# Weight chunks by half the contraction, mixer pieces behind TensorE, and expert gates applied by ScalarE

## The chip, the cores and the metric

The kernel runs on one core of a Trainium2 chip, in float32. The metric is device time in microseconds (us). Of the engines, PE is TensorE, ACT is ScalarE, DVE is VectorE, POOL is GpSimd, and SP is SyncE, which here only issues loads and stores.

## What is computed

One decoder layer for a prompt of 1024 tokens and for 8 sample tokens, at width 1024. The token mixer runs 8 retention heads and 8 dilated attention heads side by side. The channel mixer (PEER) lets each of 8 product-key heads pick 16 of 16384 single-neuron experts for each token:

```python
sh1, sc1, gt1, sh2, sc2, gt2 = adaln(c, w_ada, b_ada)
h = rmsnorm(x, g_norm1) * (1 + sc1) + sh1
rq, rk, rv, rg, aq, ak, av = mixer_projections(h, w_in, g_qn, g_kn)
o_ret, o_att, state = core(rq, rk, rv, aq, ak, av)
x = x + gt1 * mixer_output(o_ret, rg, o_att, g_ret, w_out)
h2 = rmsnorm(x, g_norm2) * (1 + sc2) + sh2
# peer, for each token and head: 16 experts eidx with scores top_s
g = softmax(top_s)
a = gelu(einsum('thkd,td->thk', peer_u[eidx], h2))
x = x + gt2 * einsum('thk,thkd->td', g * a, peer_v[eidx])
```

The outputs are x for both groups, the final retention states, and the new keys and values.

## The kernel before, in words

`build` runs three parts one after the other: `condition` (the adaLN tables), `decode` (the sample tokens up to their PEER scores) and `layer` (the prompt, and PEER for the sample at the end). The change is in `layer` alone.

`layer` works on T = 8 tiles of 128 tokens. Two streams of work are woven into each engine's one instruction list.

The PEER stream is the clock of the weave. A tile has 8 heads (HP), a head 16 expert slots, and two slots are a group (GRP = 2), so a head has 8 groups, a tile 64 (STEPS), the kernel 512. For a slot, POOL gathers a row of u and v for each of 128 tokens into a ring buffer (128 x 2048 elements, 1 MB; RING = 8 slots, four groups). DVE takes the dot product of the u half with h2 (L1395). ACT applies gelu (L965). DVE multiplies in the gate and the inverse of the softmax sum (L1411). ACT scales the v half in place (L968). PE turns it and sums it over slots in PSUM (L1134), which frees the slot for POOL (semaphore `ring_free`). While group q of head n runs, DVE also does part q of choosing the experts of head n+2 (`choose_next`). The scores of head n + AHEAD are made by PE at q = 6 and copied by ACT at q = 7.

The mixer stream is `front()`, a generator on PE, ACT and DVE each. It is cut into pieces by `yield when(t, o)`. After each group an engine runs the pieces that are due (`pace.upto`). `when` gives the group in which piece position o of tile t is due: all of tile 0 before the first group, tile 1 at o // 2, tile t from 32 groups before the start of tile t-1 on. In one tile the positions run: norm 0 to 5, input projection 6 to 19 (14 chunks of w_in, one a group, c < NIN), retention 21 to 24, attention 23 to 52 (heads in pairs, 7 groups a pair), output projection 54 to 58 (4 chunks of w_out), norm and query projection 61 to 66 (4 chunks of w_pq), queries turned at 68. In a group PE's piece comes after its transposes of that group, ACT's after its scalings, DVE's after its dots.

A chunk of weights is [128, 8, 256], that is all of the contraction for 256 columns, in one of NB = 3 buffers. SP issues chunk i when chunk i-3 has been used (L749). Its list is fixed, with the stores and the other loads in between: `load_rows` waits for the end of attention (L762), `store_y` for the sum of a tile two back (L786). `product` (L986) multiplies a chunk by eight matmuls.

At the end, the sample's experts are stored and reloaded through DRAM to have them one to a partition: DVE finishes `gate_s` in group 1 of the last head, SP stores it (L838) and loads it back in 16 small pieces (L842), POOL casts the indices (L870), gathers eight more slots (L855), and DVE, ACT and PE finish `y_sample` (L1443 to L1455).

## Time and profile before

| | us |
|---|---|
| median of 3 runs | 3926.47 |
| lowest, highest | 3908.15, 3930.04 |
| the profiled execution | 3911.71 |
| its span, first to last instruction | 3909.9 |
| PE, DVE, ACT, POOL busy | 2641.9, 2331.0, 1770.7, 1122.8 |

The mixer of tile 0 starts at 276 us; the first group ends at 441 us, the last at 3878 us. The tiles of the PEER stream end at 958, 1388, 1827, 2262, 2705, 3159, 3540 and 3878 us. DMA share is the mean busy share of 16 DMA engines; it comes out slightly above 1 where they never rest. PEclk is the clock that PE was granted, as a part of its full 2.4 GHz. A wait in brackets, as [13.14 <-DMA ...], is idle time of the engine before the instruction and what ended it.

### The profile page before, as it was taken

The page shows a single profiled execution, that of the slowest core. Times are in us where ns is not written, and L with a number is a line of the kernel's source. Part 1 is how long each engine was busy: PE and PEld are TensorE (multiplying, and loading weights), DVE is VectorE, ACT ScalarE, POOL GpSimd, SP SyncE. Part 2 cuts the span into 40 slices and gives each one's busy share as a digit, 9 for nine tenths or more (in the row PEclk, how much of TensorE's full clock was granted, in tenths as well). Part 3 has the DMA queues.
Part 4 walks back from the last instruction along what each step waited for, and adds up shares of the span by engine and source line. Part 5 has one row for each costly group of instructions (what it writes and reads, how often), then busy time and mean ns, then how long its engine had stood idle before and what let it go on. Part 6 is the DMA issues. An engine that isn't in the chain of part 4 may idle for free.

```text
span 3909.9 us, 37947 instructions
## 1 busy us (share of the span) xinstructions
PE 2641.9 (68%) x13651; PEld 2177.5 (56%) x13651; DVE 2331.0 (60%) x5816; ACT 1770.7 (45%) x2366; POOL 1122.8 (29%) x1054
## 2 busy tenths in 40 slices
PE   8777575676666766676666776676756767655555
PEld 2236464575556655565555665566655656554543
DVE  0222545457765686557765676557755577576775
ACT  0101344445544554445544554545544465454553
POOL 0000222223422233223332233322322233243443
PEclk9888786788778787787788778887778878777787
DMA  7846797899999999899999999898989999899998
GB/s 270 284 150 195 297 334 272 310 377 359 414 355 379 359 402 405 310 387 354 413 369 361 350 400 383 329 385 340 382 331 366 359 367 378 326 421 418 415 415 331
DMA packets 383772, 1373.34 MB, mean 351 GB/s; under 512 B 35168, under 2 KB 215888, under 8 KB 250208
## 3 DMA queue, kind: packets, MB, share of 16 engines
q0 software_dynamic: 149072, 1083.68, 69.6%
q1 hardware_dynamic: 234512, 287.23, 21.6%
q8 instruction: 107, 1.75, 0.2%
q14 instruction: 81, 0.66, 0.0%
HBM read 1356.74 MB, written 14.09 MB: 351 GB/s over the span
## 4 chain that ended last, share of the span: by engine, by line
PE 32%; DMA 20%; DVE 19%; ACT 18%; issue 3%; POOL 1%; DVEq 0%; POOLq 0%
PE pairA L1134 15%; PE pairS L986 12%; ACT pr_ring L968 10%; DMA pr_ring<-uv,pr_expert 10%; DVE pr_ring L1395 9%; DMA pr_w<-w_in 4%; DMA pr_w<-w_out 3%; DMA pr_w<-w_pq 3%; PE pairT L992 2%; ACT L965 2%; DVE pr_act_h L1411 1%; PE pairS L1053 1%; ACT pr_act_h L965 1%; POOL pr_ring L855 1%; ACT pr_sp L922 1%
## 5 line engine op out<-in xcount | busy, mean ns | idle before, releaser
L1134 PE MATMUL pairA<-sb_ident,pr_ring 128*128 128x128 f32 x8192 | 1389.6, 341 | 1009.7 <-ACT pr_ring L968 1006.4
L1134 PEld LDWEIGHTS pairA<-sb_ident,pr_ring 128*128 128x128 f32 x8192 | 1251.8, 180 | 1156.4 <-ACT pr_ring L968 1125.2
L855 POOL DMA_INDIRECT pr_ring<-uv,pr_expert x1024 | 1099.7, 1074 | 2492.2 <-PE pairA L1134 2175.9
L1395 DVE CUSTOM_DVE_ANT_0 pr_ring<-pr_ring,pr_h 128x1024 f32<-128x1024 f32 x1024 | 1222.6, 1222 | 135.3 <-DMA pr_ring<-uv,pr_expert 118.1
L968 ACT ACTIVATE pr_ring<-pr_ring,pr_act_h 128x1024 f32<-128x1024 f32 x1024 | 1120.1, 1141 | 157.3 <-DVE pr_act_h L1411 157.3
L986 PE MATMUL pairS<-pr_w,pr_hT 128*128 128x256 f32 x2304 | 572.3, 407 | 101.9 <-DMA pr_w<-w_in 51.8
L965 ACT ACTIVATE pr_act_h<-pr_dot 128x2 f32<-128x2 f32 x512 | 104.6, 204 | 1111.1 <-DVE pr_dot L1395 1109.2
L986 PEld LDWEIGHTS pairS<-pr_w,pr_hT 128*128 128x128 f32 x2304 | 468.9, 208 | 177.3 <-DMA pr_w<-w_pq 46.3
L1411 DVE SCALAR_TENSOR_TENSOR pr_act_h<-pr_act_h,pr_gsum,pr_gate_h 128x2 f32<-128x2 f32 x512 | 113.2, 221 | 603.8 <-ACT pr_act_h L965 603.5
L986 PE MATMUL pairS<-pr_w,pr_turned 128*128 128x256 f32 x512 | 135.4, 426 | 51.9 <-DMA pr_w<-w_out 47.4
L965 ACT ACT_TABLE_LOAD x127 | 162.9, 1283 | 2.2
L986 PEld LDWEIGHTS pairS<-pr_w,pr_turned 128*128 128x128 f32 x512 | 109.5, 219 | 71.3 <-DMA pr_w<-w_out 48.8
L1053 PE MATMUL pairS<-pr_kTva,pr_turned 64*128 64x512 f32 (+3 forms) x192 | 95.9, 614 | 6.8 <-DVE pr_st L1224 6.8
L146 PE MATMUL pairT<-ad_w,ad_cT 128*9 128x512 f32 x192 | 86.5, 605 | 9.9 <-DMA ad_w<-w_ada 9.9
L1320 DVE TENSOR_TENSOR pr_qk<-pairS,pr_rows 128x512 f32<-128x512 f32 x16 | 11.1, 692 | 133.1 <-PE pairS L986 133.1
L1222 DVE CUSTOM_DVE_ANT_0 pr_sp<-pairS,pr_dist 128x128 f32<-128x128 f32 (+7 forms) x64 | 48.4, 757 | 63.5 <-PE pairS L1053 58.9
L1395 DVE DVE_READ_ACCUMULATOR2_ANT pr_dot<- 128x1 f32 x1024 | 84.3, 82 | 0.0
L958 ACT ACT_TABLE_LOAD x64 | 82.1, 1283 | 1.1
L1192 DVE COPY pr_qk<-pairS 128x512 f32<-128x512 f32 x16 | 11.1, 692 | 106.6 <-PE pairS L986 106.6
L1068 PE MATMUL bank<-pr_kTva,pr_pt 128*128 128x65 f32 x504 | 68.8, 285 | 3.0 <-DVE pr_pt L1232 3.0
L1068 PEld LDWEIGHTS bank<-pr_kTva,pr_pt 128*128 128x128 f32 x504 | 66.6, 206 | 7.0 <-DVE pr_pt L1232 5.6
L1338 DVE MAX8 pr_top<-pr_work 128x8 f32<-128x128 f32 (+2 forms) x195 | 65.7, 337 | 4.6
(276 smaller groups left out, 1965.2 us busy)
## 6 DMA issues: line engine op xcount, KB each, us to landing
pr_w<-w_in SPq DMA_DIRECT2D x112, 1024.0 KB, 14.8
pr_w<-w_out SPq DMA_DIRECT2D x32, 1024.0 KB, 26.3
pr_w<-w_pq SPq DMA_DIRECT2D x32, 1024.0 KB, 18.8
ad_w<-w_ada SPq DMA_DIRECT2D x12, 2048.0 KB, 7.9
pr_ring<-uv,pr_expert POOLq DMA_INDIRECT x1024, 9.7
de_w<-w_in SPq DMA_DIRECT2D x7, 2048.0 KB, 11.0
...
de_kv<-k_sel SPq DMA_DIRECT2D x4, 1024.0 KB, 11.8
```

What stands on the lines that cost most here:

```text
L146: last = pe.matmul(ps[c % 2][0:NC9, :], cT[:, k, :], w[c % WBUF][:, k, :], start=(k == 0), stop=(k == KT - 1))
L855: pool.indirect_dma_start(ring[r][:], None, a["uv"], bass.IndirectOffsetOnAxis(ap=index, axis=0)).then_inc(s_g[r], 16)
L958: act.activation(gate_h[u][:], delta[u][:], ACT.Exp, accum_out=gsum[u][:, 0:1]).then_inc(s_ge, 1)
L965: act.activation(act_h[:, c], dot[:, c], ACT.Gelu).then_inc(s_gelu, 1)
L968: last = act.activation(ring[s % RING][:, D:2 * D], ring[s % RING][:, D:2 * D], ACT.Identity, scale=act_h[:, s:s + 1])
L986: last = pe.matmul(psS[:, at:at + CW], lhs[:, k, :], w[i % NB][:, k, :], start=(k == 0), stop=(k == KT - 1))
L992: last = pe.transpose(psT[:, at + k * P:at + (k + 1) * P], src[:, k * P:(k + 1) * P], ident[:])
L1053: last = pe.matmul(psS[:, c], aqT[e, h // 2, :], kT[e, h // 2, c], start=True, stop=True)
L1068: last = pe.matmul(out, pt[:, k * P:(k + 1) * P], va[:, k, h * VA:(h + 1) * VA], start=(k == 0), stop=(k == t))
L1134: last = pe.matmul(psA[:, k * P:(k + 1) * P], ring[s % RING][:, D + k * P:D + (k + 1) * P], ident[:], start=(h == 0 and s == 0 and k % 4 = ...
L1395: last = dve.tensor_tensor_reduce(ring[r][:, 0:D], ring[r][:, 0:D], h2[t % 2][:], 1.0, 0.0, ALU.mult, ALU.add, dot[:, s:s + 1])
L1411: dve.scalar_tensor_tensor(out=act_h[:, c], in0=act_h[:, c], scalar=gsum[u][:, 1:2], in1=gate_h[u][:, c], op0=ALU.mult, op1=ALU.mult)\
```

## The change

Three edits in `layer`.

Weights: a chunk is now half of the contraction for 512 columns, [128, 4, 512], still 1 MB, so that a contiguous piece of a weight row is 2 KB instead of 1 KB. The two halves of the contraction are summed in PSUM by consecutive chunks. `product` issues four matmuls of 512 columns instead of eight of 256. Number and order of the chunks stay.

Places of the pieces: tile t starts 16 groups before the start of tile t-1 instead of 32, tile 1 is at o * 3 // 4 instead of o // 2, and the positions are new. Pieces of ACT and DVE that read a result of PE are placed two groups after the PE piece that makes it. In the order of before, and with the old ranges in brackets: PE norm 1 (5), input projection 3 to 16 (6 to 19), retention 18 to 20 (21 to 23), attention 20 to 39 (23 to 52), two groups a head and no longer in pairs, output projection 41 to 46 (54 to 58), query projection 50 to 55 (62 to 66), queries turned 57, read by ACT at 59 (both 68). AHEAD is 3 instead of 4.

Gates: ACT makes the exponentials of head n+1 at group 2 of head n, DVE normalises them at group 4 (new function `gates` on each). ACT then multiplies gelu's result by the gates itself, with one 128x1 operation for each slot (scale = the gate), and waits for its own results by semaphores. DVE's L1407 and L1411 and its waits for gelu are gone. The sum of a tile (`yT`, written over `qk`) has a new wait, for PE's turning of the next tile's `qk`. The gates of the sample are made by ACT at group 2 of the last head and by DVE at group 4, instead of before group 0 and at group 1.

The core of the diff:

```diff
-    AHEAD = 4
+    AHEAD = 3
+    LEAD = 16
...
-    CW = 256
+    CK = KT // 2
...
     def when(t, o):
 
-        return -1 if t == 0 else o // 2 if t == 1 else (t - 1) * STEPS - STEPS // 2 + o
+        return -1 if t == 0 else o * 3 // 4 if t == 1 else (t - 1) * STEPS - LEAD + o
...
-        w = [sb(f"w{i}", [P, KT, CW]) for i in range(NB)]
+        w = [sb(f"w{i}", [P, CK, 512]) for i in range(NB)]
...
@@ -739,13 +741,13 @@
                 t, c = i // NCH, i % NCH
                 if i >= NB:
                     spq.wait_ge(s_pj, i - NB + 1)
+                ks, half = slice(c % 2 * CK, c % 2 * CK + CK), (c - NIN) // 2 % 2
                 if c < NIN:
-                    at = ORDER[c // 2] * HW + (c % 2) * CW
-                    src = w_in[:, :, at:at + CW]
+                    src = w_in[:, ks, ORDER[c // 2] * HW:(ORDER[c // 2] + 1) * HW]
                 elif c < NIN + 4:
-                    src = w_out[:, :, (c - NIN) * CW:(c - NIN + 1) * CW]
+                    src = w_out[:, ks, half * 512:half * 512 + 512]
                 else:
-                    src = w_pq[:, :, (c - NIN - 4) * CW:(c - NIN - 3) * CW]
+                    src = w_pq[:, ks, half * 512:half * 512 + 512]
                 spq.dma_start(w[i % NB][:], src).then_inc(s_w[i % NB], 16)
...
@@ -1069,42 +1082,35 @@
                                              va[:, k, h * VA:(h + 1) * VA], start=(k == 0), stop=(k == t))
                         last.then_inc(s_pv, 1)
 
-                    for pair in range(4):
-                        p = 23 + 7 * pair
-                        yield when(t, p)
-                        scores(2 * pair)
-                        if pair >= 1:
-                            yield when(t, p + 1)
-                            weighted(2 * pair - 1)
-                        yield when(t, p + 2)
-                        scores(2 * pair + 1)
-                        yield when(t, p + 5)
-                        turn_probs(2 * pair)
-                        yield when(t, p + 6)
-                        weighted(2 * pair)
-                        turn_probs(2 * pair + 1)
-                    yield when(t, 52)
-                    weighted(H - 1)
-
-                    yield when(t, 54)
+                    scores(0)
+                    for h in range(1, H + 2):
+                        if h < H:
+                            yield when(t, 20 + 2 * h)
+                            scores(h)
+                        yield when(t, 21 + 2 * h)
+                        if h >= 2:
+                            weighted(h - 2)
+                        if h <= H:
+                            turn_probs(h - 1)
+                    yield when(t, 41)
                     pe.wait_ge(s_mix, t + 1)
...
@@ -1273,29 +1279,21 @@
                         dve.tensor_tensor(x[:].rearrange("p (h c) -> p h c", h=H)[:, :, 0:HD], heads(osb),
                                           heads(srg), ALU.mult).then_inc(s_gated, 1)
 
-                    for pair in range(4):
-                        p = 23 + 7 * pair
-                        yield when(t, p + 1)
-                        if pair == 0:
-                            ret_out()
-                            center()
+                    for h in range(H + 1):
+                        if h < H:
+                            yield when(t, 22 + 2 * h)
+                            if h == 0:
+                                ret_out()
+                                center()
+                            att_max(h)
+                        yield when(t, 23 + 2 * h)
+                        if h == 0:
+                            deviation()
                         else:
-                            att_weigh(2 * pair - 1)
-                        att_max(2 * pair)
-                        if pair == 0:
-                            yield when(t, p + 2)
-                            deviation()
-                        yield when(t, p + 3)
...
@@ -950,27 +951,39 @@
 
             pace = Pace(front())
             pace.upto(-1)
+            def gates(n):
+                act.wait_ge(s_top, n + 1)
+                act.activation(gate_h[n % 2][:], delta[n % 2][:], ACT.Exp,
+                               accum_out=gsum[n % 2][:, 0:1]).then_inc(s_ge, 1)
+
             for n in range(AHEAD):
                 scores_out(n)
+            gates(0)
             for n in range(N):
                 u = n % 2
-                act.wait_ge(s_top, n + 1)
-                act.activation(gate_h[u][:], delta[u][:], ACT.Exp, accum_out=gsum[u][:, 0:1]).then_inc(s_ge, 1)
-                if n == N - 1:
-                    act.wait_ge(s_tops, 1)
-                    act.activation(gate_s[:], delta_s[:], ACT.Exp, accum_out=gsum_s[:, 0:1]).then_inc(s_ges, 1)
+                act.wait_ge(s_gn, n + 1)
                 for q in range(GROUPS):
-                    act.wait_ge(s_dot, n * GROUPS + q + 1)
+                    j = n * GROUPS + q
+                    act.wait_ge(s_dot, j + 1)
                     c = slice(q * GRP, q * GRP + GRP)
                     act.activation(act_h[:, c], dot[:, c], ACT.Gelu).then_inc(s_gelu, 1)
-                    act.wait_ge(s_coef, n * GROUPS + q + 1)
+                    act.wait_ge(s_gelu, j + 1)
+                    for s in range(q * GRP, q * GRP + GRP):
+                        last = act.activation(act_h[:, s:s + 1], act_h[:, s:s + 1], ACT.Identity, scale=gate_h[u][:, s:s + 1])
+                    last.then_inc(s_coef, 1)
+                    act.wait_ge(s_coef, j + 1)
                     for s in range(q * GRP, q * GRP + GRP):
                         last = act.activation(ring[s % RING][:, D:2 * D], ring[s % RING][:, D:2 * D], ACT.Identity,
                                               scale=act_h[:, s:s + 1])
                     last.then_inc(s_dg, 1)
+                    if q == 2 and n + 1 < N:
+                        gates(n + 1)
+                    if q == 2 and n == N - 1:
+                        act.wait_ge(s_tops, 1)
+                        act.activation(gate_s[:], delta_s[:], ACT.Exp, accum_out=gsum_s[:, 0:1]).then_inc(s_ges, 1)
                     if q == 7 and n + AHEAD < N:
                         scores_out(n + AHEAD)
-                    pace.upto(n * GROUPS + q)
+                    pace.upto(j)
 
...
@@ -981,9 +994,10 @@
             def product(t, c, lhs):
                 i = t * NCH + c
                 pe.wait_ge(s_w[i % NB], 16 * (i // NB + 1))
-                at = (c % 4 if c < NIN else (c - NIN) % 4) * CW
-                for k in range(KT):
-                    last = pe.matmul(psS[:, at:at + CW], lhs[:, k, :], w[i % NB][:, k, :],
+                at = (c // 2 if c < NIN else (c - NIN) // 2) % 2 * 512
+                for j in range(CK):
+                    k = c % 2 * CK + j
+                    last = pe.matmul(psS[:, at:at + 512], lhs[:, k, :], w[i % NB][:, j, :],
                                      start=(k == 0), stop=(k == KT - 1))
                 last.then_inc(s_pj, 1)
...
@@ -1376,6 +1374,12 @@
                 if part == 7:
                     dve.tensor_copy(expert[u][:], expert_f[:]).then_inc(s_top, 1)
 
+            def gates(n):
+                u = n % 2
+                dve.wait_ge(s_ge, n + 1)
+                step(dve.reciprocal(gsum[u][:, 1:2], gsum[u][:, 0:1]))
+                dve.tensor_scalar(gate_h[u][:], gate_h[u][:], gsum[u][:, 1:2], None, ALU.mult).then_inc(s_gn, 1)
+
             PARTS = 8
             assert PARTS == GROUPS
             pace = Pace(front())
@@ -1384,6 +1388,8 @@
             for n in range(2):
                 for part in range(PARTS):
                     choose_next(part, n)
+                if n == 0:
+                    gates(0)
 
             for n in range(N):
                 t, h, u = n // HP, n % HP, n % 2
@@ -1395,34 +1401,29 @@
                         last = dve.tensor_tensor_reduce(ring[r][:, 0:D], ring[r][:, 0:D], h2[t % 2][:], 1.0, 0.0,
                                                         ALU.mult, ALU.add, dot[:, s:s + 1])
                     last.then_inc(s_dot, 1)
-                    if q == 0:
-                        if h == 0 and t >= 1:
-                            dve.wait_ge(s_free, n * GROUPS)
-                            dve.wait_ge(s_owk, 16 * min(t + 2, T))
-                            if t >= T - 1:
-                                dve.wait_ge(s_oxm, 16 * T)
-                            dve.tensor_tensor(yT, psA[:].rearrange("p (k i) -> p k i", k=KT),
-                                              tabs[:, 5, :, B:B + 1].to_broadcast([P, KT, P]), ALU.mult).then_inc(s_yT, 1)
-                        dve.wait_ge(s_ge, n + 1)
-                        step(dve.reciprocal(gsum[u][:, 1:2], gsum[u][:, 0:1]))
-
-                    dve.wait_ge(s_gelu, n * GROUPS + q + 1)
-                    c = slice(q * GRP, q * GRP + GRP)
-                    dve.scalar_tensor_tensor(out=act_h[:, c], in0=act_h[:, c], scalar=gsum[u][:, 1:2],
-                                             in1=gate_h[u][:, c], op0=ALU.mult, op1=ALU.mult)\
-                       .then_inc(s_coef, 1)
+                    if q == 0 and h == 0 and t >= 1:
+                        dve.wait_ge(s_free, n * GROUPS)
+                        if t + 1 < T:
+                            dve.wait_ge(s_T, 15 * (t + 1) + 2)
+                        dve.wait_ge(s_owk, 16 * min(t + 2, T))
+                        if t >= T - 1:
+                            dve.wait_ge(s_oxm, 16 * T)
+                        dve.tensor_tensor(yT, psA[:].rearrange("p (k i) -> p k i", k=KT),
+                                          tabs[:, 5, :, B:B + 1].to_broadcast([P, KT, P]), ALU.mult).then_inc(s_yT, 1)
+                    if n + 2 < N:
+                        choose_next(q, n + 2)
                     if q == 0 and h == 0 and t >= 1:
                         dve.wait_ge(s_xmid, 16 * t)
                         dve.wait_ge(s_yb, t)
                         dve.tensor_tensor(xmid[:], psA[:], xmid[:], ALU.add).then_inc(s_out, 1)
-                    if n + 2 < N:
-                        choose_next(q, n + 2)
+                    if q == 4 and n + 1 < N:
+                        gates(n + 1)
                     if n == N - 2:
                         choose(q, ROWS_S, sc_s, delta_s, expert_s)
                         if q == GROUPS - 1:
                             dve.sem_inc(s_tops, 1)
                             dve.sem_inc(s_gts, 1)
-                    if n == N - 1 and q == 1:
+                    if n == N - 1 and q == 4:
                         dve.wait_ge(s_ges, 1)
                         step(dve.reciprocal(gsum_s[:, 1:2], gsum_s[:, 0:1]))
                         dve.tensor_scalar(gate_s[:], gate_s[:], gsum_s[:, 1:2], None, ALU.mult).then_inc(s_gts, 1)
```

## Rows read from the trace of the kernel before

**Rows 1.** Page, parts 1, 2, 3 and 6: busy, slices, queues, one issue
```profile
PE 2641.9 (68%) x13651; PEld 2177.5 (56%) x13651; DVE 2331.0 (60%) x5816; ACT 1770.7 (45%) x2366; POOL 1122.8 (29%) x1054
...
DMA  7846797899999999899999999898989999899998
...
q0 software_dynamic: 149072, 1083.68, 69.6%
...
q1 hardware_dynamic: 234512, 287.23, 21.6%
...
pr_w<-w_out SPq DMA_DIRECT2D x32, 1024.0 KB, 26.3
```

**Rows 2.** Windows: length, busy of PE, PEld, DVE, ACT, POOL; PEclk, DMA share, GB/s
```profile
276.00:441.00 165.00, 116.76 (x504) 96.03 (x504) 57.02 (x169) 29.28 (x54) 7.77 (x8) 0.77 0.64 216
441.00:958.00 517.00, 351.33 (x1854) 308.19 (x1855) 289.81 (x738) 232.60 (x316) 130.45 (x126) 0.79 0.89 330
958.00:3540.00 2582.00, 1751.44 (x9611) 1543.17 (x9611) 1687.34 (x4223) 1302.72 (x1713) 818.69 (x768) 0.79 0.96 371
3540.00:3878.00 338.00, 186.53 (x1044) 165.62 (x1042) 239.14 (x595) 175.91 (x229) 145.80 (x127) 0.76 0.99 405
```

**Rows 3.** Windows, shorter stretches, same columns
```profile
0.00:60.00 60.00, 50.06 (x127) 11.20 (x128) 0.00 (x0) 5.06 (x8) 0.20 (x4) 1.00 0.89 319
1705.00:1770.00 65.00, 54.33 (x316) 49.16 (x316) 37.34 (x92) 32.19 (x44) 17.60 (x19) 0.87 1.02 385
1549.00:1594.00 45.00, 27.05 (x117) 23.93 (x118) 25.09 (x56) 19.23 (x25) 10.82 (x10) 0.66 0.88 321
1777.00:1817.00 40.00, 25.93 (x138) 22.63 (x137) 32.18 (x81) 21.02 (x24) 11.70 (x12) 0.72 0.79 289
3560.00:3800.00 240.00, 128.70 (x726) 114.19 (x724) 173.66 (x439) 125.91 (x163) 109.94 (x91) 0.77 1.01 415
```

**Rows 4.** Timeline 1595 to 1636 us: start, us, instruction [idle before <-releaser]
```profile
1595.35 0.37 SPq L749 DMA_DIRECT2D pr_w<-w_pq  x1
...
1620.61 6.14 PE L986 MATMUL pairS<-pr_w,pr_hT 128*128 128x256 f32 x16 [13.14 <-DMA pr_w<-w_pq]
...
1626.79 0.60 ACT L939 ACTIVATE pr_sp<-pairS 128x512 f32<-128x512 f32 x1 [18.29 <-PE pairS L986]
...
1627.51 0.22 DVE L1411 SCALAR_TENSOR_TENSOR pr_act_h<-pr_act_h,pr_gsum,pr_gate_h 128x2 f32<-128x2 f32 x1 [16.97 <-ACT pr_act_h L965]
...
1635.22 0.20 ACT L883 ACTIVATE pr_st<-pr_st 128x1 f32<-128x1 f32 x1
```

**Rows 5.** Lines by form: busy us, mean ns | idle before, releaser
```profile
L968 ACT ACTIVATE pr_ring<-pr_ring,pr_act_h 128x1024 f32<-128x1024 f32 x1024 | 1120.1, 1141 | 157.3 <-DVE pr_act_h L1411 157.3
...
L965 ACT ACT_TABLE_LOAD x127 | 162.9, 1283 | 2.2
...
L1411 DVE SCALAR_TENSOR_TENSOR pr_act_h<-pr_act_h,pr_gsum,pr_gate_h 128x2 f32<-128x2 f32 x512 | 113.2, 221 | 603.8 <-ACT pr_act_h L965 603.5
...
L1222 DVE CUSTOM_DVE_ANT_0 pr_sp<-pairS,pr_dist 128x1024 f32<-128x1024 f32 x8 | 9.8, 1225 | 9.4 <-PE pairS L1053 8.1 <-issue 1.3
```

**Rows 6.** Timeline of PE in the last tile's attention
```profile
3121.85 3.78 PE L1053 MATMUL pairS<-pr_kTva,pr_turned 64*128 64x512 f32 x4
...
3125.56 3.67 PE L1134 MATMUL pairA<-sb_ident,pr_ring 128*128 128x128 f32 x16
...
3155.20 1.98 PE L1053 MATMUL pairS<-pr_kTva,pr_turned 64*128 64x512 f32 x4
...
3157.11 1.97 PE L1134 MATMUL pairA<-sb_ident,pr_ring 128*128 128x128 f32 x16
...
3158.91 1.90 PE L1068 MATMUL bank<-pr_kTva,pr_pt 128*128 128x65 f32 x16
```

**Rows 7.** Timeline at the end, SP and POOL
```profile
3843.16 0.47 SPq L838 DMA_DIRECT2D gate_s<-pr_gate_s  x1
...
3873.70 0.19 POOL L870 CAST pr_expT<-pr_expT_f 128x8 uint32<-128x8 f32 x1 [12.70 <-DMA pr_gateT<-gate_s]
```

80 lines of the change are left out of this document (37 added, 43 removed).

## The prediction

> **What bounds the kernel now.** I read the page's slices and queues first. The 16 DMA engines are at nine tenths in nearly every slice after the fifth, while no compute engine is above 68% over the span [rows 1]. Two queues share them: the gathers of expert rows (1083.68 MB, 69.6% of the span) and SP's queue with the weights (287.23 MB, 21.6%) [rows 1]. Then the windows by stage. The last tile of tokens runs almost without mixer work: 338 us for 64 groups, 5.28 us each, at a DMA share of 0.99 and 405 GB/s; an inner stretch of it gives 1.01 and 415 GB/s, which is what a full DMA looks like here [rows 2, 3]. The six tiles before it take 2582 us at 0.96, the first 517 us at 0.89 [rows 2]. So there are two costs to take away: idle DMA time (4% of 2582 us and 11% of 517 us, 103 + 57 = 160 us against a share of 1.00), and DMA time spent badly on small packets. Everything else can gain only through these.
>
> Where the DMA idles is seen inside the second tile: 1549 to 1594 us at 0.88 (output and query products), 1777 to 1817 at 0.79 (start of attention), while the input product, at 1705 to 1770, has 1.02 [rows 3]. One stall shows how it comes about [rows 4]. SP issues a chunk of w_pq at 1595.35. PE has nothing to do without it for 13.14 us and starts the product at 1620.61, 25 us after the issue. ACT stands in its own piece, waiting 18.29 us for that product, and DVE stands 16.97 us at L1411 for ACT's gelu. Meanwhile nobody frees a ring slot, and when the four groups in the ring have landed the DMA has only weights. Over the run DVE waits 603.5 us at L1411 in 505 places [rows 5].
>
> **The change part by part.**
>
> *Weight chunks.* A chunk stays 1 MB, but its packets are 2 KB, not 1 KB. SP's queue costs 0.216 x 3909.9 = 844.5 us for 287.23 MB, 2.94 us per MB, a mean that holds larger packets too. Weights with 2 KB packets are seen in the first 60 us: 0.89 x 60 us for 319 GB/s x 60 us = 19.1 MB, 2.79 us per MB [rows 1, 3]. The least saving is 0.15 us per MB on the 184.5 MB of the 176 chunks, 28 us. If the queue's other 103 MB cost 2.6, between that and the gathers' 0.696 x 3909.9 / 1083.68 = 2.51, the 1 KB packets cost 3.13 and the saving is 0.34, 62 us. I take 0.25 us per MB or 0.26 per chunk: it lies between, since the other 103 MB have small pieces too. 118 chunks fall in the six tiles (five times 22, and 8), 36 in the first: 30 + 9 us. The 22 of the opening stretch count nothing: the DMA share is 0.64 there [rows 2].
> The same edit changes when a chunk lands. Median landing of w_out is 26.3 us although 1 MB needs 3 us of the engines [rows 1]; that fits engines taking packets of the two queues in turn, each small one waiting for a large one. Half as many packets then wait half as often: I estimate 13 to 16 us for the 25 us of [rows 4]. The chunk is wanted three groups after its issue, 3 x 5.2 = 16 us, so the stalls of PE nearly go.
> The Trainium skill (DMA: Bandwidth & Descriptors, Queues, rings and completion order) says that an engine goes round the queues at packet granularity; the landing time agrees. The same page (Specifications) puts line rate at 512 B and more, by which 1 KB packets have nothing to gain; the rows, 2.94 against 2.79 us per MB, speak mildly against it. It is a rival below.
> PE's work per chunk stays: half the matmuls, each twice as long. The weight loads halve, but they run beside the matmuls (56% and 68% of the span, together over 100% [rows 1]): nothing.
>
> *Gates in ScalarE.* DVE loses 512 x 0.221 us = 113 us and the 603.5 us of waiting [rows 5]. It is not bound: about 72% busy without mixer work (173.66 of 240 us [rows 3]). What it gains is that a late ACT no longer holds up DVE's next dots or its mixer piece. ACT gains two 128x1 operations per group; nearest row 0.20 us each [rows 4]. It used to stand 157.3 / 512 = 0.31 us there for DVE [rows 5]. The chain from dots to scaled values is then gelu + 0.40 + two short waits on itself, against gelu + 0.31. Bounds: -0.1 us (they overlap) to +0.5 us per group. At the path it is nothing at either end, because gathers queue: a slot's data is awaited by a DMA at 0.99 and not by ACT. Without that cover 0.5 x 512 would be 256 us. The softmax sum is applied one head ahead (groups 2 and 4), with no more table loads.
>
> *Pieces two groups behind.* PE's piece of a group comes after its transposes, so ACT and DVE, who are ahead, waited for it in the same group. Now the readers sit two groups (10.6 us) later. Attention takes 20 groups for 30 and the whole mixer 59 for 68. Is there room? Per head and two groups, at 128 x 1024: DVE has 3.7 x 2 (72% of 5.28, twice) + 1.225 for the maximum [rows 5] + as much for the weighing, of the same shape + 0.2 = 10.1 us. ACT has 2 x (0.2 + 0.4 + 2.2) + 1.14 + two table loads of 1.283 = 9.3 (each head's exponential now changes the table by itself, where two shared a change). PE at full clock has 2 x 1.97 + 1.98 + 1.0 + 1.90 = 8.8 [rows 6]. The DMA needs 2 x 5.28 = 10.6, and more where w_out is loaded. It fits, narrowly for DVE in the last tile. Queued behind each moved piece are that engine's next dots, scalings or transposes; the ring of four groups covers some 10 us. SP's store_y finds its tile ready earlier (group 16 for 32), so the w_out loads behind it come earlier, into the attention stretch that idles now. The new DVE wait, for PE's turning of qk before yT is written over it, is on a piece due six groups before: nothing. AHEAD 3 for 4 leaves ACT's scores one group and more ahead of DVE: nothing.
> I take that the six tiles reach a share of 0.99: (2582 x 0.96 - 30) / 0.99 = 2449 / 0.99 = 2474, -108 us. The first tile has a mixer pressed into 44 groups, of which two per three stay on time: share 0.97, (517 x 0.89 - 9) / 0.97 = 465, -52 us. The last tile is full already: 0.
>
> *Start and end.* At the start choose(1) now waits for the first gates (a table load, 1.28, and small operations, some 2 us), against 2 us that larger packets may give between products: 0. At the end the sample's gates are made at group 4 of the last head instead of group 1. Their store (3843.16) begins the chain to POOL's cast at 3873.70, where POOL stood 12.70 us idle [rows 7]; the sample's eight gathers and the end of the kernel hang on it. Three groups x 5.28 = 15.8 later; the gathers no longer share the DMA: +14, bounds +10 and +16.
>
> *Sum.* -108 - 52 + 14 = -146. The profiled execution took 3911.7 us, so 3765.7. It is 0.4% below the median of the three runs, 3926.5, and near their lowest; I keep to it: **3765 us**.
>
> **The rivals.**
> 1. *Packets gain nothing*, since the engines move 1 KB pieces as fast as larger ones. The 39 us stay: 2479 / 0.99 = 2504 (-78), 460 / 0.97 = 474 (-43), +14: **3805**. (That is what the line rate of the Trainium skill's DMA page would give.) For it: the difference in rows is small and the 2 KB stretch has no gathers beside it.
> 2. *New waits for old.* Chunks still land late, because the alternation is only inferred, or DVE's 10.1 of 10.6 us makes late groups in attention. Half the idle time comes back: shares 0.975 and 0.92, 2449 / 0.975 = 2512 (-70), 451 / 0.92 = 490 (-27), +14: **3829**.
> 3. *The reordering does nothing*: shares as now, only packets, -39 + 14: **3887**, which is faster by 0.6% and with packets at their least (-22 + 14) no change. Against it: the stall of [rows 4] is plainly one of order and landing.
> 4. *Slower: PE at its low clock in the denser attention.* The granted clock averages 0.77 to 0.79 [rows 2], a mix of the two levels 2.4 and 1.2 GHz; the same 16 transposes take 1.97 or 3.67 us [rows 6]. At the low level a head of the last tile costs PE 3.78 + 1.8 + 3.8 + 2 x 3.67 = 16.8 us in two groups against 10.6 of DMA; with keys growing by tile the excess sums to about 19 us per head position, 154 us over eight heads. If then also the stalls stay, 3887 + 154 = **4041**; I put it at 3980. It decides the sign where PE's two groups average above 10.6 + 146 / 48 = 13.6 us over the six upper tiles. Against it: in [rows 6] PE is at the full level when its pieces follow each other without a gap, and the change makes them denser.
>
> **How the numbers follow.** Forecast 0.62, rival 1 0.10, rival 2 0.18, rival 3 0.04, rival 4 0.06. The predicted time is the forecast's. Its own range: shares 1.01 and 1.00 with 62 us of packets, (2479 - 41) / 1.01 = 2414 and 447, -168 - 70 + 12 gives 3686; the upper end is rival 1, 3805. The whole range takes rival 2 with some of its spread: **3690 to 3850**. A measurement can tell about 0.5% from no change, 20 us. Faster by more than that: 0.62 + 0.10 + 0.18 and half of rival 3, 0.90 with a little off for what I don't see; same 0.04; slower 0.06.
>
> **What would show it.** DMA share of the six middle tiles at 0.98 or more, with under 2474 + 20 us for them; median landing of w_out under 18 us; PE's waits on weights far under the present ones; ACT's wait on projections gone; DVE's wait on gelu gone with nothing of its size in its place; the sample's gathers some 15 us later against the last group. I am wrong if the share stays at 0.96, if landing stays near 26 us, if SP's cost per MB doesn't fall, or if PE's 3.67 us transposes fill the attention stretches.

## The result

The changed kernel takes 3596.31 us in the median of four runs (3593.3 to 3606.4); the kernel before, measured beside it, 3917.31 us (3902.18 to 3930.04). The ratio is 0.9186, 95% interval 0.9143 to 0.923: 321 us, or 8.1%, faster. Forecast were 3765 us and a range of 3690 to 3850, so the sign is right and the size is not: the gain is twice the one predicted, and the time lies 94 us below the range.

The page of the kernel after has the same parts as [rows 1]: busy time, the DMA's slices, the queues (packets, MB, share of 16 engines' span), and the median landing of the weight chunks, with two groups of ScalarE that the change touches.

```profile
span 3591.5 us, 35730 instructions
...
PE 2546.8 (71%) x12243; PEld 1797.8 (50%) x12243; DVE 2251.8 (63%) x5368; ACT 2046.4 (57%) x3415; POOL 1168.4 (33%) x1054
...
DMA  8736699999999999999999999999999999999998
...
q0 software_dynamic: 149072, 1083.68, 73.6%
q1 hardware_dynamic: 144400, 287.23, 21.7%
...
L972 ACT ACTIVATE pr_act_h<-pr_act_h,pr_gate_h 128x1 f32<-128x1 f32 x1024 | 245.8, 287 | 16.9
L969 ACT ACT_TABLE_LOAD x136 | 174.5, 1283 | 16.2 <-DVE pr_dot L1401 13.8
...
pr_w<-w_in SPq DMA_DIRECT2D x112, 1024.0 KB, 17.5
pr_w<-w_out SPq DMA_DIRECT2D x32, 1024.0 KB, 20.4
pr_w<-w_pq SPq DMA_DIRECT2D x32, 1024.0 KB, 23.6
```

The bytes are the same, 1083.68 and 287.23 MB; q1 moves them in 144400 packets where [rows 1] has 234512. In time, q0 is 0.736 x 3591.5 = 2643 us (before 0.696 x 3909.9 = 2721) and q1 0.217 x 3591.5 = 779 us (before 844.5). What is left of the span, when the two queues' time is taken off, is 169 us where it was 344; I call it idle time. So the 318 us between the two spans are three things: the DMA is less idle (175), the weights' packets cost less (65), and the gathers' packets, of which the change touches none, cost less too (78).

The windows by stage answer to [rows 2]: opening stretch, first tile, six middle tiles, last tile, end; columns as there.

```profile
276.00:439.00 163.00, 113.14 (x328) 59.61 (x328) 56.42 (x166) 28.39 (x51) 7.63 (x8) 0.78 0.64 221
439.00:865.00 426.00, 313.41 (x1478) 218.60 (x1477) 270.09 (x662) 263.65 (x443) 138.90 (x126) 0.84 1.00 398
865.00:3222.00 2357.00, 1690.63 (x8756) 1281.43 (x8754) 1642.26 (x3913) 1516.05 (x2508) 860.08 (x769) 0.83 1.00 406
3222.00:3560.00 338.00, 194.65 (x1042) 173.43 (x1042) 225.30 (x535) 207.74 (x356) 143.26 (x127) 0.73 0.99 405
3560.00:3592.00 32.00, 17.64 (x41) 3.39 (x40) 15.74 (x28) 1.62 (x8) 4.58 (x5) 0.87 0.64 256
```

The six tiles fell from 2582 to 2357 us and from 0.96 to 1.00, the first from 517 to 426 and from 0.89 to 1.00. The last tile is 338 us in both kernels and the opening stretch is 2 us shorter. From the first group to the last the kernel now moves 398 to 406 GB/s.

The table of waits (engine, line, what it waited for: total us, times, longest us) shows who waits in a kernel that the DMA bounds. First the kernel before, then the kernel after.

```profile
POOL pr_ring L855 <- PE pairA L1134: 2175.9, 499, 18.6
...
DVE pr_ring L1395 <- DMA pr_ring<-uv,pr_expert: 118.1, 127, 2.7
...
PE pairS L986 <- DMA pr_w<-w_in: 51.8, 15, 7.9
...
PE pairS L986 <- DMA pr_w<-w_out: 47.4, 6, 12.6
...
PE pairS L986 <- DMA pr_w<-w_pq: 44.9, 6, 13.1
```

```profile
POOL pr_ring L857 <- PE pairA L1140: 1806.2, 466, 20.1
ACT pr_act_h L969 <- DVE pr_dot L1401: 958.6, 379, 16.1
...
DVE pr_ring L1401 <- DMA pr_ring<-uv,pr_expert: 658.9, 519, 5.4
...
PE pairS L1000 <- DMA pr_w<-w_in: 139.9, 41, 6.7
...
PE pairS L1000 <- DMA pr_w<-w_pq: 31.9, 7, 5.6
...
PE pairS L1000 <- DMA pr_w<-w_out: 29.0, 7, 6.5
```

DVE's wait for ScalarE's gelu, 603.5 us in [rows 5], is gone. In its place DVE waits 658.9 us for the gathered rows themselves (118.1 before), in 519 places with 5.4 us at most: the first compute engine on a row stands ready before the data, and the DMA does not idle for it. PE's waits for weights are not gone. In total they have grown, from 144 us in 27 places to 201 us in 55; but no single one is over 6.7 us, against 13.14 in [rows 4].

### The profile page after: what moved, and what is told of

Same layout as the page of the kernel before. It is cut to its first block, busy times and chain, and to the rows that moved or that the text cites. A ratio compares the mean times of both kernels' runs of the same rounds, so it can differ in the third digit from the quotient of the medians.

```text
span 3591.5 us, 35730 instructions
## 1 busy us (share of the span) xinstructions
PE 2546.8 (71%) x12243; PEld 1797.8 (50%) x12243; DVE 2251.8 (63%) x5368; ACT 2046.4 (57%) x3415; POOL 1168.4 (33%) x1054
## 3 DMA queue, kind: packets, MB, share of 16 engines
q0 software_dynamic: 149072, 1083.68, 73.6%
q1 hardware_dynamic: 144400, 287.23, 21.7%
## 4 chain that ended last, share of the span: by engine, by line
DMA 42%; PE 23%; ACT 12%; DVE 9%; POOL 4%; issue 3%; POOLq 0%; DVEq 0%; ACTq 0%
DMA pr_ring<-uv,pr_expert 23%; PE pairS L1000 12%; DMA pr_w<-w_in 12%; PE pairA L1140 9%; ACT pr_ring L976 6%; DVE pr_ring L1401 5%; POOL pr_ring L857 4%; DMA pr_w<-w_pq 3%; DMA pr_w<-w_out 3%; ACT pr_act_h L972 1%; ACT L969 1%; ACT L923 1%; ACT pr_act_h L969 1%; PE pairT L1006 1%; PE bank L1081 0%
## 5 line engine op out<-in xcount | busy, mean ns | idle before, releaser
L857 POOL DMA_INDIRECT pr_ring<-uv,pr_expert x1024 | 1146.5, 1120 | 2129.6 <-PE pairA L1140 1806.2
L1140 PE MATMUL pairA<-sb_ident,pr_ring 128*128 128x128 f32 x8192 | 1286.3, 324 | 733.7 <-ACT pr_ring L976 723.2
L1401 DVE CUSTOM_DVE_ANT_0 pr_ring<-pr_ring,pr_h 128x1024 f32<-128x1024 f32 x1024 | 1242.2, 1224 | 671.1 <-DMA pr_ring<-uv,pr_expert 658.9
L1140 PEld LDWEIGHTS pairA<-sb_ident,pr_ring 128*128 128x128 f32 x8192 | 1167.6, 170 | 918.8 <-ACT pr_ring L976 843.1
L1000 PE MATMUL pairS<-pr_w,pr_hT 128*128 128x512 f32 x1152 | 594.5, 667 | 180.0 <-DMA pr_w<-w_in 139.9
L969 ACT ACTIVATE pr_act_h<-pr_dot 128x2 f32<-128x2 f32 x512 | 104.1, 203 | 960.1 <-DVE pr_dot L1401 958.6
L1000 PEld LDWEIGHTS pairS<-pr_w,pr_hT 128*128 128x128 f32 x1152 | 238.3, 216 | 455.1 <-issue 339.4
L972 ACT ACTIVATE pr_act_h<-pr_act_h,pr_gate_h 128x1 f32<-128x1 f32 x1024 | 245.8, 287 | 16.9
L1000 PE MATMUL pairS<-pr_w,pr_turned 128*128 128x512 f32 x256 | 132.6, 669 | 31.2 <-DMA pr_w<-w_out 29.0
L1000 PEld LDWEIGHTS pairS<-pr_w,pr_turned 128*128 128x128 f32 x256 | 52.9, 216 | 92.6 <-issue 58.3
L1337 DVE FIND_INDEX8 pr_pos<-pr_top,pr_work 128x8 uint32<-128x128 f32 (+2 forms) x195 | 64.2, 329 | 0.0
L1006 PE MATMUL pairT<-sb_ident,pr_sp 128*128 128x128 f32 x352 | 58.8, 302 | 5.7 <-ACT pr_sp L923 5.0
## 6 DMA issues: line engine op xcount, KB each, us to landing
pr_w<-w_in SPq DMA_DIRECT2D x112, 1024.0 KB, 17.5
pr_w<-w_out SPq DMA_DIRECT2D x32, 1024.0 KB, 20.4
pr_w<-w_pq SPq DMA_DIRECT2D x32, 1024.0 KB, 23.6
```

The source lines that it names most:

```text
L857: pool.indirect_dma_start(ring[r][:], None, a["uv"], bass.IndirectOffsetOnAxis(ap=index, axis=0)).then_inc(s_g[r], 16)
L969: act.activation(act_h[:, c], dot[:, c], ACT.Gelu).then_inc(s_gelu, 1)
L972: last = act.activation(act_h[:, s:s + 1], act_h[:, s:s + 1], ACT.Identity, scale=gate_h[u][:, s:s + 1])
L1000: last = pe.matmul(psS[:, at:at + 512], lhs[:, k, :], w[i % NB][:, j, :], start=(k == 0), stop=(k == KT - 1))
L1006: last = pe.transpose(psT[:, at + k * P:at + (k + 1) * P], src[:, k * P:(k + 1) * P], ident[:])
L1140: last = pe.matmul(psA[:, k * P:(k + 1) * P], ring[s % RING][:, D + k * P:D + (k + 1) * P], ident[:], start=(h == 0 and s == 0 and k % 4 = ...
```

## The experiments

Two theories of the gathers' cheaper packets are to be told apart. By the one (theory B in the expectations below) they are served faster because the weights' packets between them are fewer and larger; by the other (theory A) because the DMA has fewer gaps. The other questions are what each part is worth alone and beside the others, why the sum was too small, and why the tail's +14 us is missing.

Of each experiment the profiled span P is split as above: q0 and q1 are their shares times P, the rest is P less both. The packet times are means of the packet records in each trace, in ns: a gather packet of 8 KB, and a packet of a weight chunk with its size. P is one execution. That of e_places was the slowest of its four, 17 us above their median, that of e_1kb 8 us above, so their rest is high by up to so much. Gains in us below are differences of the ratios times 3917, unless other numbers stand there, because the kernels ran on several chips.

```
kernel            ratio   95% interval      P       q0    q1   rest  gather  weight packet
before            1                         3909.9  2721  845  344   327.9   49.6 (1 KB)
after             0.9186  0.9143 to 0.923   3591.5  2643  779  169   318.6   88.6 (2 KB)
e_chunks          0.9747  0.9694 to 0.9799  3818.1  2711  787  320   326.6   2 KB
e_places          0.9572  0.9528 to 0.9616  3766.3  2678  844  245   322.9   1 KB
e_gates           0.9957  0.9924 to 0.9991  3907.4  2716  844  348   327.5   1 KB
e_places_gates    0.949   0.9448 to 0.9532  3709.9  2656  842  212   320.1   1 KB
e_chunks_places   0.9143  0.9093 to 0.9194  3605.1  2661  779  166   320.5   2 KB
e_chunks_gates    0.966   0.9608 to 0.9711  3807.8  2707  784  316   326.5   2 KB
e_1kb             0.9493  0.9417 to 0.9568  3735.5  2656  848  231   319.9   49.8 (1 KB)
e_512b            0.9748  0.9671 to 0.9824  3822.7  2668  963  191   321.3   29.8 (512 B)
e_ring3           0.9796  0.9693 to 0.9899  3834.0  2764  786  284   333.2   2 KB
e_nolag           1.1828  1.1736 to 1.192   4641.8  2767  784  1091  333.6   2 KB
```

**Each part alone.** Three kernels, each the kernel before with one of the three parts of the change. Chunks (e_chunks):

```diff
-        w = [sb(f"w{i}", [P, KT, CW]) for i in range(NB)]
+        w = [sb(f"w{i}", [P, CK, 512]) for i in range(NB)]
...
-                    src = w_out[:, :, (c - NIN) * CW:(c - NIN + 1) * CW]
+                    src = w_out[:, ks, half * 512:half * 512 + 512]
```

> The kernel before with one part of the change: weight chunks of half the contraction by 512 columns, 2 KB packets. Places of pieces and gates as before. Theory A (gaps): the change gained mostly by closing gaps in the DMA's work, and gather packets took 329 ns on average instead of 318 because the DMA ran empty now and then; then this kernel keeps most gaps, gather packets stay above 325 ns, and it gains 40 to 90 us, around 3850. Theory B (contention): the 1 KB packets slow the gathers beside them; then gather packets fall to about 318 ns here already, and it gains 140 us or more, 3780 or less.

It took 3815.87 us, ratio 0.9747: 99 us faster, a little more than theory A allowed (40 to 90), and well short of theory B's 140. q1 fell by 58 us, q0 by 10, the rest by 24. The gathers' packets stay at 326.6 ns, though the weights' packets beside them are now 2 KB. So larger weight packets beside them are not what makes the gathers cheaper. With the old places the median landing of w_out falls to 19.6 us and that of w_pq to 15.4.

Places (e_places): the positions of all pieces on PE, ACT and DVE as in the diff, with AHEAD 3; chunks and gates as before.

```diff
-                    yield when(t, 54)
+                    yield when(t, 41)
                     pe.wait_ge(s_mix, t + 1)
```

> The kernel before with one part of the change: the new places of the mixer pieces (with AHEAD 3 and the wait before the sum of a tile). Chunks of 256 columns, gates multiplied in by DVE. Theory A: most of the gain is here, 150 to 220 us, around 3730, and the middle tiles reach a rate near 395 GB/s. Theory B: the stalls removed count for at most the idle share, about 100 us, 3815.

3751.52 us, ratio 0.9572: 168 us faster. Here q1 does not move (844 for 845) and the weights' packets are the old ones, but q0 falls by 43 us and the rest by 99. The gather packet falls from 327.9 to 322.9 ns in a kernel in which nothing was done to any packet. What this kernel changed is how seldom the DMA runs out of gathers. It does not say how the 168 us divide between the readers' distance of two groups, the denser attention and the later start: no kernel here has the distance with the old order.

Gates (e_gates): the gates multiplied in by ScalarE, with AHEAD 3 and everything else at its old place. In this kernel the scores of the last head of a tile are made from other queries than the reference's; the amount and the kind of the work are the same, only the rows that are gathered differ.

```diff
+                    act.wait_ge(s_gelu, j + 1)
+                    for s in range(q * GRP, q * GRP + GRP):
+                        last = act.activation(act_h[:, s:s + 1], act_h[:, s:s + 1], ACT.Identity, scale=gate_h[u][:, s:s + 1])
+                    last.then_inc(s_coef, 1)
```

> The kernel before with one part of the change: gates made one head ahead and multiplied in by ScalarE (with AHEAD 3, which it needs to start). Chunks and places as before. My account gives it little alone: ScalarE still stands waiting for TensorE in its pieces, so the slots are freed as late; DVE gains only its 1.2 us per group. 0 to 60 us, around 3885. A rival: DVE held up by ScalarE was the main cause of the gaps; then 120 us or more.

3910.58 us, ratio 0.9957, 0.9924 to 0.9991: 17 us at the most likely, and little more than can be told from nothing. Taking away DVE's 603.5 us of waiting for ACT gave no more than that, so these waits were hardly on the path.

**The parts in pairs.** 168 + 99 + 17 = 284 us, and the change, counted the same way, gives 319. Three more kernels leave one part out each.

> The changed kernel without its weight chunks: 256 columns and all of the contraction, 1 KB packets; places and gates as changed. Theory A: the DMA stays full, the gathers' packets stay at 318 to 320 ns, and only the packets of the weights cost more, 45 to 65 us: 3640 to 3665. Theory B: gather packets go back to 325 ns or more and it loses 120 us or more: 3720.

3714.31 us, ratio 0.949. Leaving the chunks out costs 119 us of the 319. The gather packets stay at 320.1 ns, as theory A has it and B (325 or more) has not. But A's price of 45 to 65 us was too low by half, and the time is nearly B's: q1 rises by 63 us, q0 by 13, and the idle time by 43. PE's waits on weights show where the last comes from.

```profile
PE pairS L999 <- DMA pr_w<-w_in: 199.8, 28, 13.3
...
PE pairS L999 <- DMA pr_w<-w_out: 92.3, 7, 14.2
...
PE pairS L999 <- DMA pr_w<-w_pq: 88.4, 7, 14.7
```

Together 380 us, the longest 14.7; in the kernel after they are 201 us and 6.7. With the denser places a chunk has less time before it is wanted. In 1 KB packets PE stands up to 14.7 us for one, once in each of seven tiles for w_out and for w_pq and 28 times for w_in.

> The changed kernel without its gates: DVE multiplies them in and waits for gelu again; chunks and places as changed. Without the chunks the gates were worth 37 us beside the new places. Theory A: about the same here, 25 to 45 us, 3630. Rival: with the DMA full there is nothing left for them, under 10 us, 3600.

3605.81 us, ratio 0.9143: the whole gain without the gates, as the rival had it. To compare it with the full change, both ran again on one chip.

> The changed kernel once more, to stand beside the next three on the same chip: 3590 to 3600, 0.915 to 0.922 of the kernel before.

> The changed kernel without its gates, once more beside it: the first time it stood at 0.914 on another chip, against 0.919 for the change. Theory A (with the DMA full, nothing is left for DVE and ACT to give): within 8 us of the changed kernel. Rival: 20 us or more slower, as the 37 us beside 1 KB packets say.

The full change took 3600.9 us, 0.9185 (0.9147 to 0.9222), the same without the gates 3607.78, 0.921 (0.9172 to 0.9248). The gates are worth 7 us there, inside both intervals. Where the DMA still idles they are worth more: 32 us beside the places alone (0.9572 to 0.949), and 34 beside the chunks alone (0.9747 to the 0.966 below).

The last pair keeps the old places. AHEAD is 4 again here, so that each tile's scores come from its own queries, and the first gates stand between the first score copies:

```diff
             for n in range(AHEAD):
                 scores_out(n)
+                if n == 1:
+                    gates(0)
```

> The changed kernel without its places: old positions and lead, AHEAD 4; chunks and gates as changed. Chunks alone gave 105 us, gates alone 17 us. If the parts add up: 3800, so that the places are worth 200 us on top of the others. If gates and chunks help each other (ACT and DVE no longer tied, chunks landing sooner), 3750 or less.

3808.23 us, ratio 0.966. The parts add up about as expected. Against the whole change this is 0.966 to 0.9186: the new places are worth some 185 us when the chunks and the gates are there, and 168 alone.

**The size of a weight packet.** The kernel after, with each chunk loaded in two column halves (packets of 1 KB) or four quarters (512 B). PE's work and every place stay.

```diff
-                spq.dma_start(w[i % NB][:], src).then_inc(s_w[i % NB], 16)
+                for s in range(2):
+                    cs = slice(s * 512 // 2, (s + 1) * 512 // 2)
+                    spq.dma_start(w[i % NB][:, :, cs], src[:, :, cs]).then_inc(s_w[i % NB], 16)
```

> The changed kernel with one thing back: each weight chunk is fetched by two loads of 256 columns into the same buffer, so its packets are 1 KB again; chunks, products, places and gates stay. Theory A: what the chunks gave is the packet size and nothing else, so it costs what the full undoing of the chunks cost, 118 us: 3700 to 3720, with SP's queue at about 840 us of the 16 engines and gather packets near 320 ns. Rival: half the contraction and TensorE's 512 columns gave a part; then it stays below 3680.

3729.12 us, ratio 0.9493. It is the same as e_places_gates with its 0.949, which has 1 KB packets in one load for each chunk: so the packets count, and neither the number of loads nor the shape of PE's product. Against the kernel after it is 120 us by the two ratios and 144 by the spans: q1 69, q0 13, rest 62 (43 in e_places_gates). The waits of PE for weights are twice those of the kernel after:

```profile
PE pairS L1002 <- DMA pr_w<-w_in: 224.5, 23, 13.9
...
PE pairS L1002 <- DMA pr_w<-w_pq: 94.8, 7, 14.7
PE pairS L1002 <- DMA pr_w<-w_out: 93.7, 7, 14.1
```

> As the last one, with four loads of 128 columns for a chunk, 512 B packets. From 49.6 ns at 1 KB and 88.6 ns at 2 KB a packet costs some 10.6 ns plus 38 ns per KB, so 30 ns at 512 B and 3.67 us per MB against 3.03: +118 us of DMA time above the 1 KB kernel, and more late chunks: 3830 to 3900. The rule that line rate begins at 512 B (the Trainium skill, DMA: Bandwidth & Descriptors, Specifications) would give the time of the 2 KB kernel, 3600.

3823.96 us, ratio 0.9748, with 272.0 + 116.7 + 105.9 = 495 us of such waits, the longest 17.7. q1 costs 115 us more than in e_1kb, and the kernel takes 100 more: part of it falls into idle time, which sinks from 231 to 191. So the columns of the table are no independent prices. A packet of 512 B takes 29.8 ns, of 1 KB 49.8, of 2 KB 88.6. A chunk of 1 MB on 16 engines then costs 3.82, 3.19 and 2.84 us with 2^20 bytes, or 3.64, 3.04 and 2.70 us for 10^6. The Trainium skill (DMA: Bandwidth & Descriptors, Specifications) puts line rate at 512 B and more. These runs disagree: between 512 B and 2 KB lie 35% in engine time and, by the ratios 0.9748 and 0.9186, 220 us of the kernel's. That was rival 1 of the prediction, and it falls.

**The distance between PE and its readers.** The kernel after, with the pieces of ACT and DVE moved back into the group of PE's piece that they read (two groups earlier, PE's places untouched).

```diff
                     for h in range(H):
-                        yield when(t, max(23, 22 + 2 * h))
+                        yield when(t, max(21, 20 + 2 * h))
                         act.wait_ge(s_nm, t * H + h + 1)
```

> The changed kernel with the pieces of ACT and DVE that read TensorE moved two groups forward, into the group of the TensorE piece that they read. TensorE's own places, the denser attention, the lead of 16 groups, chunks and gates stay. Theory A: the distance of two groups is what closes the gaps; it loses 80 to 150 us, 3700. Rival: the later start, the packing and the decoupled gates do it, and the ring covers such waits; under 30 us, 3620.

4642.73 us, ratio 1.1828: 716 us slower than before, 1035 slower than after. The sign was expected; the loss is some seven times the upper end that I wrote down. Its waits:

```profile
POOL pr_ring L857 <- PE pairA L1140: 2906.7, 451, 17.6
...
DVE pr_pt L1238 <- PE pairT L1006: 387.2, 64, 10.0
DVE pr_sp L1228 <- PE pairS L1066: 379.6, 53, 12.7
...
ACT pr_sp L923 <- DVE pr_st L1230: 272.4, 55, 8.0
```

64 and 53 times, once a head, DVE stands 6 to 7 us for PE, and ACT 5 us for DVE. In the stretch from 1700 to 1800 us the DMA share is 0.55 at 204 GB/s. The old order spread a pair of heads over seven groups; at two groups a head such waits come one behind the other. So the denser order pays only with the distance. That the ring's four groups cannot cover waits that come so close is my reading of it; no run changes the ring in this order.

**Gathers under way.** Does a gather's packet take longer because the DMA has gaps? The kernel after, with POOL allowed three groups in the ring and not four:

```diff
-                    if s % GRP == 0 and j >= RING // GRP:
-                        pool.wait_ge(s_free, j - RING // GRP + 1)
+                    if s % GRP == 0 and j >= RING // GRP - 1:
+                        pool.wait_ge(s_free, j - RING // GRP + 2)
```

> The changed kernel with three groups of gathers under way instead of four: POOL waits for one more freed group. No other change, packets of weights 2 KB. It tests whether gaps alone lengthen the gathers' packets: if so their mean rises from 318.6 ns to 325 ns or more while the time grows by over 100 us. If the mean stays at 318 to 320, the longer packets of the kernel before came from something else. The ring's cover goes too: I expect 3750 to 3900.

3843.86 us in the median of two runs, ratio 0.9796. Its queues, from the page, and a window in its last tile (same columns as the windows above):

```profile
q0 software_dynamic: 149072, 1083.68, 72.1%
q1 hardware_dynamic: 144400, 287.23, 20.5%
```

```profile
3560.00:3780.00 220.00, 118.78 (x580) 106.35 (x580) 128.18 (x307) 119.32 (x206) 83.79 (x73) 0.67 0.93 347
```

q0 is 0.721 x 3834.0 = 2764 us, 121 more than after, for the same bytes in the same packets, and the gather packet is 333.2 ns, above even the 327.9 of before, beside weight packets of 2 KB. In the window a share of 0.93 moves 347 GB/s, 2.68 us of DMA time per MB; the full stretch in [rows 3] moves 415 at 1.01, 2.43. So the busy share hides a loss: when fewer gathers are under way, the engines' records still show them busy, with longer packets. The total of idle time is not what sets it: e_ring3 has less than the kernel before (284 us for 344) and dearer packets, and e_nolag, with 1091, has no dearer ones than e_ring3.

The packet records say more than the means. The median gather packet takes 309 to 313 ns in every kernel of the table. What differs is how many take over 400 ns, some 700 on average: 1.26% after, 3.58% before, 2.50% in e_places, 5.14% in e_ring3, 5.21% in e_nolag. Without these the mean is 313.8 ns before and after alike, so they are all of the 78 us: what they cost above that mean is 117 us before and 39 after. They come where the engines had begun to run dry. From 400 to 3500 us of each run, of the gather packets that start when the 16 engines were less than 0.8 busy in the 400 ns before, 44 to 68 in 100 are long (after, before, e_ring3, e_nolag); of those that start at 0.97 or more, 1 to 3 in 100. From the first group to the last, the packets that start at less than 0.9 are 1.0% of the gathers after, 3.5% before, 5.4% in e_ring3 and 5.7% in e_nolag, the order of the means. So it goes by how often the engines run dry and not by how long. More than half of the long packets start at 0.9 or more all the same (in e_nolag just under half), and what delays those the records don't say.

**The tail.** The kernel after, with the sample's gates made at the first group of the last head:

```diff
-                    if q == 2 and n == N - 1:
+                    if q == 0 and n == N - 1:
...
-                    if n == N - 1 and q == 4:
+                    if n == N - 1 and q == 1:
```

> The changed kernel with the sample's gates made early again: ACT after group 0, DVE at group 1 of the last head. My prediction priced the later place at 14 us; in the changed trace the small loads behind it took 16.5 us from the store to POOL's cast, where they took 30.5 us before. Theory: those loads wait for the gathers' traffic to end either way, so this kernel is the same within 3 us, 3594 to 3599. If the price was real and hidden by something else, it gains 10 us or more.

3591.91 us, ratio 0.9103 (0.9052 to 0.9153): not to be told from the change itself. SP's timeline says why: first the kernel before, then the kernel after, then e_tail (start, us, instruction).

```profile
3848.77 4.51 SPq L842 DMA_DIRECT2D pr_expT_f<-expert_s  x8
3853.33 15.33 SPq L842 DMA_DIRECT2D pr_gateT<-gate_s  x8
```

```profile
3538.66 0.47 SPq L840 DMA_DIRECT2D gate_s<-pr_gate_s  x1
3544.53 3.74 SPq L844 DMA_DIRECT2D pr_expT_f<-expert_s  x8
3548.31 4.65 SPq L844 DMA_DIRECT2D pr_gateT<-gate_s  x8
```

```profile
3532.24 0.47 SPq L840 DMA_DIRECT2D gate_s<-pr_gate_s  x1
3538.12 3.66 SPq L844 DMA_DIRECT2D pr_expT_f<-expert_s  x8
3541.82 16.34 SPq L844 DMA_DIRECT2D pr_gateT<-gate_s  x8
```

The store is earlier, but the eight small loads of the gates then take 16.34 us to issue and not 4.65. They were as long before the change too (15.33 us). What the two slow cases have in common is that POOL still issues gathers of the prompt beside them (until 3551.8 in e_tail, 3861.0 before), while in the kernel after its last one is at 3544.1. It can't be the gathers alone, for the eight loads just ahead of them take 3.7 to 4.5 us in all three. POOL's cast, at the end of that chain, stands 5.9 us ahead of the last release of a slot in e_tail and 5.0 us ahead in the kernel after.

**Where the mixer of the next tile starts.** Most of the idle time that is left in the middle tiles lies at a tile's start. The windows at two of them in the kernel after:

```profile
2060.00:2100.00 40.00, 31.22 (x178) 23.07 (x179) 28.07 (x68) 20.48 (x35) 11.89 (x12) 0.87 0.78 304
...
2860.00:2900.00 40.00, 30.93 (x175) 22.66 (x176) 27.63 (x67) 20.48 (x35) 13.49 (x12) 0.87 0.81 309
```

0.78 and 0.81, where the windows of 40 us on both sides have 1.02. In the first of them a w_in chunk is late behind its predecessor, and the PEER work of every engine is queued behind it (start, us, instruction, idle before and what ended it):

```profile
2062.96 6.25 PE L1000 MATMUL pairS<-pr_w,pr_hT 128*128 128x512 f32 x8 [6.38 <-DMA pr_w<-w_in]
...
2070.19 1.22 DVE L1418 TENSOR_TENSOR pr_xmid<-pairA,pr_xmid 128x1024 f32<-128x1024 f32 x1 [12.35 <-PE pairA L1134]
```

L1134 and L1418 are the last steps of a tile of the PEER stream: its output is turned and added, which comes on top of the mixer's work when both fall in one group. With LEAD 18 or 20 for 16 the mixer's pieces stand two or four groups further from the tile's end.

```diff
-    LEAD = 16
+    LEAD = 18
```

> The changed kernel with a lead of 18 groups instead of 16, one number. In the changed trace three tiles begin with 53 to 55 us for 8 groups at a DMA share of 0.85 to 0.93, the others with 46 to 47: TensorE has the last two products of w_in just before and after turning the tile's sum, and waits for a late chunk with DVE and the ring behind it. With 18 these products come before the sum. If that is the cause, 10 to 25 us faster than the changed kernel; if the tile's end costs this anyway, within 5 us.

> The same with a lead of 20: the sum of a tile then falls in the first group of attention. If only the distance from the products counts, as e_lead18; if the heavy retention pieces at positions 20 to 22 meet the sum, slower than e_lead18 by 5 to 15 us.

On the chip of r_after (3600.9 us), LEAD 18 took 3587.42, ratio 0.9156 (0.912 to 0.9193), and LEAD 20 3589.87, 0.9153 (0.9116 to 0.919). Both came out as the distance from the products has it. The intervals overlap with r_after's, but they hold the noise of the kernel before; of the six runs of r_after on the same chip, five are above all six of LEAD 18 and all six of LEAD 20. So there is most likely a gain, and it is one of 11 to 13 us. The stretches in question, in e_lead18:

```profile
2020.00:2060.00 40.00, 29.99 (x135) 18.36 (x134) 11.90 (x21) 17.04 (x27) 10.64 (x10) 0.88 0.87 343
...
2820.00:2860.00 40.00, 31.20 (x131) 18.79 (x132) 12.72 (x24) 17.03 (x27) 9.70 (x10) 0.87 0.90 360
```

0.87 and 0.90, and a third at 0.91 near 2420: the gaps are shallower, but the picture is another one, for DVE is busy 12 us in these 40 where it was 28. So LEAD moves the stall and softens it; it doesn't take it away.

## Why the prediction was wrong

**Right.** The DMA bounds the kernel, and the gain came out of its idle time and its small packets. The last tile stayed at 338 us. ScalarE's extra work cost nothing at the path although I sized it too small: 0.48 us per group for the two 128x1 operations, 287 ns each in the page above, where I took 0.40 from the 0.20 of [rows 4] (that row's operation has no scale read from a tile). The Trainium skill (ScalarE: Activation LUTs, What ACT_TABLE_LOAD costs) adds some 93 ns for each operand that is read from a 128x1 tile; 287 ns against the 203 of the gelu at L969, a difference of 84, agrees. "Nothing of its size" in place of DVE's wait on gelu was a sign that failed, since 658.9 us of waiting for rows came, but they cost nothing. Rival 4 did not come: PEclk rose from 0.79 to 0.83 in the six tiles. My argument against it was weaker than I wrote, though: [rows 6] also has 3.78 and 3.67 us, at the low level, one right behind the other. Rival 3 falls with e_places (168 us from the reordering alone), rival 1 with e_1kb and e_512b, and rival 2 with the shares of 1.00.

**The step that failed: DMA idle time read off the busy share.** I wrote that there are two costs, "idle DMA time (4% of 2582 us and 11% of 517 us [...])" and packets, and that everything else can gain only through these. But the share was not the measure of what was left. The rows had it: the six tiles moved 371 GB/s where a full stretch moves 415 [rows 2, 3]. By bytes the floor is 2582 x 371 / 415 = 2308 us, 274 us below, and not the 103 us that the share allowed; they now take 2357 us at 406 GB/s. (2308 is a little too low: the stretch at 415 holds almost only gathers.) For the first tile 517 x 330 / 415 = 411, measured 426. The stretch of [rows 3] at 0.79 moved 289 GB/s, 2.73 us per MB against 2.43 for the full one: the sign that packets take longer in a DMA that runs with gaps. I used the row for the share alone. It is 78 us of q0 that my sum had no term for, all of it in the few per cent of gather packets that take over 400 ns; e_places shows it without any change of packets, e_ring3 brings it back. The share was also rounded: 0.96 is 0.955 in the packet records, so that 117 us were idle in the six tiles and 58 in the first, 175 and not 160, and all of them went (3 us and nothing are left).

**The term of the packets was mis-sized, twice.** I took 0.25 us per MB, 39 us for seven tiles, with 62 as the most. q1 fell by 65 us in the pair of kernels, 58 in e_chunks, 69 in e_1kb against after. The upper bound was nearly the truth and I took the middle, because the mean of queue 1 and the first 60 us were the rows at hand. Per MB, 1 KB packets cost 3.04 us and those of 2 KB 2.70, a difference of 0.34. The opening stretch also counted nothing, though its packets cost as much. And I had counted the landing of a chunk only as a help to reach 0.99. It is a term of its own: 43 and 62 us of idle time lie between the two 1 KB versions and the 2 KB version of the kernel after. My estimate of the landing, 13 to 16 us for the 25 us of [rows 4], and under 18 for w_out's median, was wrong in the number (w_out 20.4; the medians of w_in and w_pq even rose, from 14.8 to 17.5 and from 18.8 to 23.6). The new places lengthen the landing and the larger packets shorten it, w_pq excepted: with the new places and 1 KB (e_places_gates) the medians of w_in, w_out and w_pq are 20.0, 28.2 and 22.6. So halving the packets took w_out down by a quarter and not by half. I also gave PE's waits on weights as a sign, "far under the present ones", and that sign failed: 201 us for 144. Only the longest wait shows the help: 13.1 before, 14.7 with the new places and 1 KB, 6.7 with 2 KB.

**The shares.** 0.99 and 0.97 were forecast, 1.00 and 1.00 came. Within my own way of counting that is 25 us for the six tiles and 14 for the first. "It fits, narrowly" was the right reading of DVE's work in 10.6 us, and it fits with nothing lost, even though 72% of 5.28 us is 3.8 and not 3.7, so that 10.3 should have stood for 10.1.

**The tail.** +14 us did not come. The step took it that the chain starts when the store starts. Before the change the chain's small loads took 15.33 us beside the gathers; after it 4.65. From the store to POOL's cast it was 30.5 us, and now it is 16.5: what the later start took, the shorter chain gave back. e_tail undoes the one and gets the other.

**The sum again.** Forecast were -108 for the six tiles, -52 for the first, +14 and 0. Measured are -225, -91, 0 (32 us in the end window in both) and -2: -318. By cause and not by place: idle time -175 where I had -121 (78 and 43), weight packets -65 where I had -39, gather packets -78 where I had nothing, and the tail 0 where I had +14.

What stays open: what inside the DMA makes a gather packet beside a gap take 700 ns for 310, how the gain of the places divides among its parts, and why the eight loads of the gates are slow in two kernels and fast in one.
